# A fused two-block kernel: weight slots of 2,096 words in place of 2,080, so that the second slot begins 64 bytes off its former place modulo 128

## The chip, the cores and the metric

One core of a Trainium2 chip runs one program. The metric is device time in microseconds (us) of one execution; lower is better.

## The reference, cut to what matters

Two transformer blocks run one after the other on 256 tokens of width 1024, all in float32. Nearly all the arithmetic is in products with weight matrices:

```python
proj = rms_norm(x, g) @ w_in                                  # first block: 3 mixers' inputs, gates
mixed = g_a*(o_a @ w_up_a) + g_b*(o_b @ w_up_b) + g_c*(o_c @ w_up_c)
x = x + mixed @ w_out
x = x + (silu(h @ w_gate) * (h @ w_up)) @ w_down              # 1024 -> 2816 -> 1024
...
x = x + 0.5 * swiglu(rms_norm(x), w_gate, w_up, w_down)       # second block: twice, round a mixer
```

The mixers between them (top-k attention, a gated recurrence, latent attention, forgetting attention, stick-breaking attention) are small beside the weights, of which some 185 MB are read.

## The kernel before

The activations stand transposed, 128 features on the partitions and the 256 tokens along the row. The weights come as 189 tiles (`TILES`), most of them 1 MB: 128 partitions by 2,048 words, which is two blocks of 128 output columns by 8 slices of the contraction. The tiles of the down projections (`w_dn`) have 1,408 words, and two of them make one output block. Tile g uses slot g % 2 of three buffers that stand one behind the other in a partition:

```python
SLOT = 4 * FVL                              # L43; FVL = 520, so 2,080 words or 8,320 bytes
raw = fixed("raw", (2, SLOT))               # L352: as loaded
whi = fixed("whi", (2, SLOT), F32R)         # L353: rounded to fp32r
wlo = fixed("wlo", (2, SLOT), F32R)         # L354: raw - whi, what the rounding left
...
mm(bank[:, 0:T], hi, h[:, 0:T], first, False)        # L685: whi x high half of activations
mm(bank[:, 0:T], hi, h[:, T:2 * T], False, False)    # L686: whi x low half
return mm(bank[:, 0:T], lo, h[:, 0:T], False, last)  # L687: wlo x high half
```

SyncE (SP) loads a tile into `raw` (L631) once VectorE has split the tile that had the slot. ScalarE copies `raw` to `whi` (`split_high`, recorded at L1179), in halves, VectorE subtracts into `wlo` (`split_low` L1575, and L1663 in the loops over the gate and up weights), and TensorE then runs three matmuls for each slice of the contraction (`one_region`, all recorded at L681). In nearly all of them the weights are the stationary operand, of 128 columns, and 256 columns of the activations are the moving one (`hs`, `hid`, `ms`, `osplit_a` to `osplit_c`, `osplit_fox`, `osplit_sb`, `cqs`, `ckvs`, `ps`). In five kinds of tiles the roles are exchanged (`block_n`): the weights are streamed, 136 columns at a time (`w_avw`) or 512 (`w_bi`, `w_kvb`, `w_fvl`, `w_sv`), against stationary activations. In `w_avw` and `w_fvl` the rows of a slice have 136 and 520 words, so that four slices running begin 0, 32, 64 and 96 bytes off modulo 128. The last 8 columns of a `w_fvl` slice are stationary in matmuls of their own, 128x8 against 256 moving columns of `hs`.

The order of the work on each engine is written out by hand (`order_of_work`, L194 on), with loops for the gate and up weights (`w_gu`) and the down weights; no place in it depends on `SLOT`.

`fixed` lays tensors out from the lowest free address, each rounded up to 64 bytes. In the built program `x` begins at byte 16,512 of a partition, 129 times 128, and `raw`, `whi` and `wlo` follow at multiples of 128 too. 8,320 is 65 times 128, so slot 1 of each also begins at a multiple of 128. Behind them come `tmp`, `con` and others. The large area of the activations (`arena`) and `hs` begin 64 bytes off modulo 128: all moving operands named above do.

Of the kernel before, what the change touches and what calls it, by code (L numbers as in the profile page):

```python
# [39 lines left out]
LB_FLOOR = 1e-30  # L40
AVW = P + IDX_H
FVL = FOX_H * HD + FOX_H
SLOT = 4 * FVL  # L43
ARENA = 29024


# [283 lines left out]
def build(nc, a, out_t):  # L330

    with ExitStack() as ctx:
# [13 lines left out]
        def fixed(name, shape, dt=F32):  # L346
            off = top[0]
            top[0] += (4 * int(np.prod(shape)) + 63) // 64 * 64
            return at(name, shape, off, dt)

        x = fixed("x", (KD, T))
        raw = fixed("raw", (2, SLOT))  # L352
        whi = fixed("whi", (2, SLOT), F32R)  # L353
        wlo = fixed("wlo", (2, SLOT), F32R)  # L354
        tmp = fixed("tmp", (4, T))
# [1992 lines left out]
```

How the kernel before makes its waits and increments, by code:

```python
        @block.sync  # L613
        def _(sp):
            f, e = FIRST_CONST, EARLY_CONST
            xT = a["xT"].rearrange("k p t -> p k t")
            for piece in range(KD // 2):
                c = slice(2 * piece, 2 * piece + 2)
                sp.dma_start(x[:, c, :], xT[:, c, :]).then_inc(S(f"x_loaded{piece}"), 16)
            sp.dma_start(vec[:], a["vecs"]).then_inc(S("vec_loaded"), 16)
            sp.dma_start(raw[:, 0, 0:TILES[0][2]], a["w_projT_a"][0]).then_inc(S("w_loaded0"), 16)
            half = TILES[1][3]
            sp.dma_start(raw[:, 1, 0:half], a["w_projT_a"][1][:, 0:half]).then_inc(S("w_loaded1a"), 16)
            sp.wait_ge(S(f"x_loaded{KD // 2 - 1}"), 16)
            sp.dma_start(raw[:, 1, half:TILES[1][2]], a["w_projT_a"][1][:, half:]).then_inc(S("w_loaded1"), 16)
            sp.dma_start(con[:, f:e], a["consts"][:, f:e]).then_inc(S("con_loaded"), 16)
            sp.dma_start(con[:, e:], a["consts"][:, e:]).then_inc(S("masks_loaded"), 16)
# [1 line left out]
            def load(src, slot, n, lo_needed):  # L629
                sp.wait_ge(S("w_lo"), lo_needed)
                sp.dma_start(raw[:, slot, 0:n], src).then_inc(S(f"w_loaded{slot}"), 16)
# [8 lines left out]
            def place_bias(tt):  # L640
                sp.wait_ge(S("bias_staged"), tt + 1)
                ks, c0 = P * (tt + 1), P * tt
                for m in range(4):
                    sp.dma_start(bias[m::4, :, c0:c0 + ks], stage[tt][:, ks * m:ks * m + ks])\
                        .then_inc(S("bias_placed"), 16)
```

## Time and profile before

| | us |
|---|---|
| median of three runs | 1059.9 |
| lowest, highest | 1058.3, 1060.31 |
| span of the profiled execution, first to last instruction | 1057.7 |
| median run less that span | 2.2 |
| TensorE busy, of the span | 1047.9 (99%) |
| VectorE busy | 741.0 (70%) |
| ScalarE busy | 579.6 (55%) |
| HBM read | 184.98 MB |

No time of the profiled execution other than its span is among the figures; the 2.2 us stand for what lies around a span. In the profile, "PE" is a matmul and "PEld" the load of a stationary operand, which runs beside the matmul before it. Matmuls are pipelined: each is recorded as some 276 ns long, but the next begins long before that. What counts is the distance from start to start, called spacing here.

### The profile page before, as it was taken

What the parts mean: (1) busy time and instruction counts of PE and PEld (TensorE: products, weight loads), DVE (VectorE), ACT (ScalarE), POOL (GpSimd) and SP (SyncE); (2) the same over time, 40 slices, a digit from 0 to 9 for tenths busy, and PEclk for the clock granted to TensorE, in tenths of its full rate; (3) what the DMA queues carried; (4) which work ended last, traced back from release to release, by engine and by line L of the source; (5) the groups of instructions that cost most, each with busy time, mean ns of one, the idle gap of its engine ahead of it and who ended that gap; (6) DMA issues with size and microseconds to landing.
All of it is one profiled execution on the core that took longest, in us unless ns stands there. A gap on an engine that the chain in (4) does not pass through costs nothing.

```text
span 1057.7 us, 22212 instructions
## 1 busy us (share of the span) xinstructions
PE 1047.9 (99%) x8760; PEld 1020.3 (96%) x8760; DVE 741.0 (70%) x1098; ACT 579.6 (55%) x880; POOL 77.0 (7%) x92
## 2 busy tenths in 40 slices
PE   9999999999999999999999999999999999999998
PEld 8899999999999999999999999898889999999998
DVE  6799988747876666657666677667986876665666
ACT  5456655576565544556544445455666664554553
POOL 0000000001310000111000001041001300000110
PEclk9999999999999999999999999999999999999999
DMA  6356433344556554555555456464335455554563
GB/s 235 129 173 217 162 123 120 120 160 170 190 181 217 190 186 146 198 204 190 205 196 194 148 193 217 173 207 162 137 120 199 171 191 196 198 203 146 195 222 120
DMA packets 32444, 187.81 MB, mean 178 GB/s; under 512 B 3832, under 2 KB 7552, under 8 KB 14720
## 3 DMA queue, kind: packets, MB, share of 16 engines
q1 hardware_dynamic: 31472, 185.58, 50.3%
q0 software_dynamic: 416, 1.06, 0.4%
q8 instruction: 43, 0.70, 0.3%
q10 hardware_dynamic: 496, 0.33, 0.2%
q14 instruction: 17, 0.14, 0.0%
HBM read 184.98 MB, written 1.06 MB: 176 GB/s over the span
## 4 chain that ended last, share of the span: by engine, by line
PE 87%; DVE 6%; ACT 1%; issue 1%; DVEq 0%; ACTq 0%
PE acc L681 83%; PE area_a L681 2%; PE area_t L681 2%; DVE wlo L1575 2%; DVE s_sum L2133 0%; ACT he L1179 0%; ACT whi L1179 0%; PE area_t L947 0%; ACT s_a L1179 0%; DVE mask L1780 0%; DVE st L1765 0%; DVE score L1805 0%; DVE s_z L2135 0%; DVE s_a L2131 0%; DVE s_z L2037 0%
## 5 line engine op out<-in xcount | busy, mean ns | idle before, releaser
L681 PE MATMUL acc<-hs,whi 128*128 128x256 f32 x3584 | 624.6, 279 | 2.9 <-DVE wlo L1575 2.7
L681 PEld LDWEIGHTS acc<-hs,whi 128*128 128x128 f32 x3584 | 541.9, 187 | 10.1 <-issue 7.1
L681 PE MATMUL acc<-hs,wlo 128*128 128x256 f32 x1792 | 496.8, 277 | 0.0
L1179 ACT ACTIVATE whi<-raw 128x1024 fp32r<-128x1024 f32 (+3 forms) x379 | 357.2, 978 | 162.8 <-PE acc L681 136.6
L1575 DVE TENSOR_TENSOR wlo<-raw,whi 128x1024 fp32r<-128x1024 f32 (+4 forms) x259 | 272.1, 1092 | 98.5 <-ACT whi L1179 97.4
L681 PEld LDWEIGHTS acc<-hs,wlo 128*128 128x128 f32 x1792 | 336.1, 188 | 0.2
L681 PE MATMUL acc<-hid,whi 128*128 128x256 f32 x1056 | 180.9, 277 | 0.2 <-DVE wlo L1575 0.2
L681 PEld LDWEIGHTS acc<-hid,whi 128*128 128x128 f32 x1056 | 159.2, 188 | 0.4 <-DVE wlo L1575 0.4
L681 PE MATMUL acc<-hid,wlo 128*128 128x256 f32 x528 | 146.0, 277 | 0.0
L1663 DVE TENSOR_TENSOR wlo<-raw,whi 128x1024 fp32r<-128x1024 f32 x120 | 141.2, 1219 | 4.3 <-ACT whi L1179 4.2
L1676 DVE TENSOR_TENSOR hbuf<-acc,sbuf 128x256 f32<-128x256 f32 x66 | 28.0, 425 | 115.4 <-PE acc L681 112.0
L681 PEld LDWEIGHTS acc<-hid,wlo 128*128 128x128 f32 x528 | 99.1, 188 | 0.0
L1179 ACT ACTIVATE sbuf<-gbuf 128x256 f32<-128x256 f32 x66 | 27.6, 417 | 126.8 <-DVE gbuf L1669 126.8
L681 PE MATMUL acc<-ms,whi 128*128 128x256 f32 x256 | 44.9, 279 | 0.0
L681 PEld LDWEIGHTS acc<-ms,whi 128*128 128x128 f32 x256 | 38.8, 188 | 0.3
L681 PE MATMUL acc<-whi,hs 128*128 128x512 f32 (+1 forms) x128 | 37.4, 370 | 0.0
L2181 POOL TENSOR_TENSOR sq_sum<-sq_sum,sq_ring 128x256 f32<-128x256 f32 x30 | 28.5, 950 | 116.6 <-ACT sq_ring L1179 116.6
L2181 POOL TENSOR_TENSOR sq_sum<-sq_ring 128x256 f32<-128x256 f32 x5 | 5.0, 1000 | 435.2 <-ACT sq_ring L1179 435.2
L2169 POOL TENSOR_TENSOR mixed<-mixed,up 128x256 f32<-128x256 f32 x24 | 17.7, 771 | 250.0 <-DVE up L1605 250.0
L681 PE MATMUL acc<-ms,wlo 128*128 128x256 f32 x128 | 35.5, 278 | 0.0
L1179 ACT ACTIVATE hid<-hbuf 128x256 f32 (+1 forms) x66 | 26.5, 402 | 10.5 <-DVE hbuf L1676 10.5
L1693 DVE TENSOR_TENSOR hid<-hbuf,hid 128x256 f32 (+1 forms) x66 | 27.6, 419 | 2.9 <-ACT hid L1179 2.9
(316 smaller groups left out, 1029.2 us busy)
## 6 DMA issues: line engine op xcount, KB each, us to landing
raw<-in_w_gu SPq DMA_DIRECT2D x66, 1024.0 KB, 4.8
raw<-in_w_dn SPq DMA_DIRECT2D x48, 704.0 KB, 4.0
raw<-in_w_up SPq DMA_DIRECT2D x10, 1024.0 KB, 4.8
raw<-in_w_gates1b SPq DMA_DIRECT2D x8, 1024.0 KB, 4.7
raw<-in_w_out SPq DMA_DIRECT2D x8, 1024.0 KB, 4.8
raw<-in_w_qk SPq DMA_DIRECT2D x8, 1024.0 KB, 4.8
raw<-in_w_gates SPq DMA_DIRECT2D x8, 1024.0 KB, 4.8
raw<-in_w_projT_b SPq DMA_DIRECT2D x7, 1024.0 KB, 4.8
```

The costliest lines, as they stand in the source:

```text
L681: return nc.tensor.matmul(out, w, m, start=start, stop=stop, skip_group_check=True)
L1179: return nc.scalar.activation(out, in_, f, **kw)
L1575: m = v.tensor_tensor(to, src, hi.bitcast(F32), ALU.subtract)
L1663: v.tensor_tensor(wlo[:, 1 - j, c], raw[:, 1 - j, c], whi[:, 1 - j, c].bitcast(F32), ALU.subtract).then_inc(S("w_lo"), 1)
L1676: v.tensor_tensor(hbuf[:, j, :], acc[(n0 + 2 * j + 1) % 4][:, 0:T], sbuf[:, j, :], ALU.mult)\
L1693: v.tensor_tensor(hid[:, t - 1, T:2 * T], hbuf[:, 1 - j, :], hid[:, t - 1, 0:T].bitcast(F32), ALU.subtract).then_inc(S("hid_lo"), 1)
L2169: nc.gpsimd.tensor_tensor(mixed[:, k, :], mixed[:, k, :], up[:, u % 4, :], ALU.add)\
L2181: nc.gpsimd.tensor_tensor(sq_sum[:], before, sq_ring[:, k % 2, :], ALU.add)\
```

## The change

It makes a slot of the three buffers 16 words (64 bytes) longer. Nothing reads or writes the new words.

```diff
@@ -40,7 +40,7 @@
 LB_FLOOR = 1e-30
 AVW = P + IDX_H
 FVL = FOX_H * HD + FOX_H
-SLOT = 4 * FVL
+SLOT = 4 * FVL + 16
 ARENA = 29024
```

A slot is then 8,384 bytes, 65.5 times 128. Slot 0 of `raw` stays; slot 0 of `whi` moves up by 128 bytes and that of `wlo` by 256; all that is behind them moves by 384. Those keep their places modulo 128. Slot 1 of each of the three alone is now 64 bytes off modulo 128, which is the place of `hs` and of the activations in the arena. The instructions of every engine, their number and their order are the same in both programs.

## Rows read from the trace of the kernel before

**Rows 1.** The page: busy time, share of the span, instructions; granted TensorE clock.
```profile
PE 1047.9 (99%) x8760; PEld 1020.3 (96%) x8760; DVE 741.0 (70%) x1098; ACT 579.6 (55%) x880; POOL 77.0 (7%) x92
PEclk9999999999999999999999999999999999999999
```

**Rows 2.** The chain of waits in order of time: start us, us, what, matmuls.
```profile
118.70 5.89 PE acc L681 x48
126.38 5.66 PE acc L681 x48
133.82 5.66 PE acc L681 x48
...
303.48 174.80 PE acc L681 x1536
...
851.47 180.61 PE acc L681 x1584
```

**Rows 3.** Windows: us, each engine's busy time (x instructions), granted clock, DMA share, GB/s.
```profile
304.00:314.00 10.00, 10.00 (x87) 10.00 (x86) 8.29 (x10) 6.64 (x9) 0.00 (x0) 1.00 0.50 193
...
326.00:416.00 90.00, 90.00 (x797) 90.00 (x796) 56.77 (x85) 44.86 (x66) 0.00 (x0) 1.00 0.53 188
```

**Rows 4.** Timeline of TensorE matmuls, 313.9 to 315.2 us: start us, us, what.
```profile
313.92 0.40 PE L681 MATMUL acc<-hs,whi 128*128 128x256 f32 x2
...
314.27 0.40 PE L681 MATMUL acc<-hs,whi 128*128 128x256 f32 x2
...
314.62 0.39 PE L681 MATMUL acc<-hs,whi 128*128 128x256 f32 x2
...
314.96 0.39 PE L681 MATMUL acc<-hs,whi 128*128 128x256 f32 x2
```

**Rows 5.** Groups of instructions by line and form: count, busy us, mean ns.
```profile
L681 PE MATMUL acc<-hs,whi 128*128 128x256 f32 x3568 | 621.7, 279 | 2.9 <-DVE wlo L1575 2.7
L681 PE MATMUL acc<-hs,wlo 128*128 128x256 f32 x1784 | 494.6, 277 | 0.0
L681 PE MATMUL acc<-hid,whi 128*128 128x256 f32 x1056 | 180.9, 277 | 0.2 <-DVE wlo L1575 0.2
L681 PE MATMUL acc<-hid,wlo 128*128 128x256 f32 x528 | 146.0, 277 | 0.0
```

**Rows 6.** Timeline of TensorE matmuls: the 8-column weights of w_fvl, two places.
```profile
667.56 0.39 PE L681 MATMUL acc<-hs,whi 128*8 128x256 f32 x2
...
667.91 0.39 PE L681 MATMUL acc<-hs,whi 128*8 128x256 f32 x2
...
671.05 0.39 PE L681 MATMUL acc<-hs,whi 128*8 128x256 f32 x2
...
671.39 0.39 PE L681 MATMUL acc<-hs,whi 128*8 128x256 f32 x2
```

**Rows 7.** Groups by line and form: loads of stationary weights, 128 and 8 columns.
```profile
L681 PEld LDWEIGHTS acc<-hs,whi 128*128 128x128 f32 x3568 | 540.5, 188 | 9.1 <-issue 7.1 <-DVE wlo L1575 1.0 <-DVE qk L1607 0.2
...
L681 PEld LDWEIGHTS acc<-hs,whi 128*8 128x8 f32 x16 | 1.4, 88 | 1.0
```

**Rows 8.** Timeline of TensorE matmuls with weights moving, 512 columns, w_bi: aligned slices.
```profile
102.36 0.62 PE L681 MATMUL acc<-whi,hs 128*128 128x512 f32 x2
...
103.05 0.62 PE L681 MATMUL acc<-whi,hs 128*128 128x512 f32 x2
...
107.17 0.63 PE L681 MATMUL acc<-whi,hs 128*128 128x512 f32 x2
...
107.87 0.63 PE L681 MATMUL acc<-whi,hs 128*128 128x512 f32 x2
```

**Rows 9.** The same view in w_fvl, where slices begin 0, 32, 64, 96 bytes off.
```profile
665.23 0.63 PE L681 MATMUL acc<-whi,hs 128*128 128x512 f32 x2
...
665.93 0.63 PE L681 MATMUL acc<-whi,hs 128*128 128x512 f32 x2
...
666.63 0.62 PE L681 MATMUL acc<-whi,hs 128*128 128x512 f32 x2
```

**Rows 10.** One line's instructions: duration ns min/median/max; first and last start.
```profile
L1663 DVE TENSOR_TENSOR wlo<-raw,whi x120: 1216/1218/1227, 311.8 to 962.3; 128x1024 fp32r<-128x1024 f32 x120
```

**Rows 11.** DMA issues by tensor: count, KB each, median us from issue to landing.
```profile
raw<-in_w_gu SPq DMA_DIRECT2D x66, 1024.0 KB, 4.8
raw<-in_w_dn SPq DMA_DIRECT2D x48, 704.0 KB, 4.0
...
raw<-in_w_kvb SPq DMA_DIRECT2D x1, 1024.0 KB, 4.7
...
raw<-in_w_pp SPq DMA_DIRECT2D x1, 1024.0 KB, 4.7
```

**Rows 12.** Timeline of TensorE: transposes in plain fp32, 128 columns.
```profile
751.75 0.49 PE L947 MATMUL area_t<-con,f_p 128*128 128x128 f32 x3
```

## The prediction

> **What bounds the kernel now.** The page first: TensorE is busy for 1047.9 us of a span of 1057.7, at the full granted clock, the higher of its two levels (2.4 GHz), in every slice [rows 1]. A busy TensorE is not yet a bound, so the chain of waits comes next. It is made of runs of matmuls at line L681 that nothing interrupts: 1,536 of them in 174.80 us, 1,584 in 180.61 [rows 2]. VectorE and ScalarE are busy 70% and 55% and stand on the chain only between those runs. So the time is the number of matmuls times their spacing, plus the gaps of the mixers. The change touches no instruction; what it can alter is how fast an instruction reads or writes at its new address, and TensorE's spacing above all.
>
> The third view is that spacing. It has two values. From 326 to 416 us TensorE issues 797 matmuls in 90 us, 113 ns each; from 304 to 314 us it issues 87 in 10 us, 115 ns by count, and a few records can be missing, so the timeline is surer [rows 3]. There three matmuls (one slice) start 0.35 us after the last three up to 314.62, and 0.34 from then on [rows 4]. Over longer stretches of the same form: 48 matmuls in 5.66 us at 126.38 and 133.82, 118 ns each [rows 2]. I call them slow and fast: 118 and 113.3 ns. The reader is to see three things. The spacing changes inside an unbroken stream, at the border of a tile. It then stays: within the 90 us of fast spacing both slots were used in turn, and VectorE and ScalarE came and went (85 and 66 instructions) without moving it. And slot 1 (at 126.38, tile 17) and slot 0 (at 133.82, tile 18) both show the slow one. So what picks the spacing is neither the slot nor the neighbours; it is some phase that is set when TensorE has waited or turned to another tile.
>
> How much runs at each: of the two long runs of the chain, 1,536 in 174.80 us is 113.8 ns each and 1,584 in 180.61 is 114.0 [rows 2], so a tenth to a sixth of them is slow. In the short runs between the mixers most is, like the two of 48. I take a quarter of all as slow. The number of matmuls that matter is 3,568 + 1,784 + 1,056 + 528 = 6,936 [rows 5], and some 900 with `ms`, `osplit` and the small ones; 7,800 in all, 3,900 of them in slot 1.
>
> **The change part by part.** *Instructions:* none added, removed or moved, 0.
>
> *VectorE and ScalarE on slot 1.* They read `raw` and `whi` and write `wlo`, all three shifted by the same 64 bytes. The subtraction takes 1,216 to 1,227 ns over 120 instances, half of them in each slot [rows 10], while TensorE reads the other slot at whatever address. With the operands' places relative to each other unchanged I take 0. If each of the 188 halves that pass through slot 1 grew by 1%, 12 ns, it would be 2 us of VectorE's time, and its 30% of idle time [rows 1] covers them; without that cover they would be TensorE's.
>
> *The loads.* A tile lands 4.8 us after its issue, one of `w_dn` after 4.0 [rows 11]. Tile 23 (`w_kvb`) goes to slot 1 and tile 188 (`w_pp`) to slot 0; today these begin 128 bytes apart modulo 256, and both took 4.7 us [rows 11]. I take 0, and 5% of 4.0 us as the dearest case for the 24 tiles of `w_dn` in slot 1, 33 matmuls or 3.7 us apart, where the load has the least cover: 0.2 × 24 = 4.8 us. The page "DMA: Bandwidth & Descriptors" of the Trainium skill, section "How a descriptor splits into AXI transactions", has a read that does not start at a multiple of 256 bytes begin at the boundary below it. It speaks against the change, since slot 1 of `raw` leaves such a boundary; but slot 0 lies off one already, and the two rows above agree to 0.1 us, so the sum by the page would be the same here.
>
> *TensorE, weights moving* (`w_avw`, `w_bi`, `w_kvb`, `w_fvl`, `w_sv`). Here the trace shows other addresses. With aligned slices, three matmuls of 512 columns take 0.69 us at 102.36 and 0.70 at 107.17 [rows 8], again two values. In `w_fvl`, where the slices begin at 0, 32, 64 and 96 bytes, three take 0.70 and 0.70 [rows 9]. So all four places lie at the upper of the two values that one place alone has, and the 64 bytes make at most 0.01 us per three. There are some 130 such matmuls in slot 1: 0 taken, 0.4 us either way as the bound.
>
> *TensorE, weights stationary.* This is the term that decides, 3,900 matmuls in slot 1. The trace has no 128-column weights at 64 bytes off, so it is bounded. The nearest rows are the 8-column weights of `w_fvl`: their load takes 88 ns in place of 188 [rows 7], it reads a sixteenth of the words, and still the spacing of their matmuls is 0.35 us per three at one place and 0.34 at the next [rows 6], the same two values as with full weights. If the 6 to 11 ns above the 107 ns of the transposes [rows 12] came from the weights' reads meeting the activations' reads, they ought to have shrunk there. They did not; so I take it that they belong to the moving operand, whose address modulo 128 the change leaves alone. I take 0 because these rows are nearest. Above, the bound is that all of slot 1 goes slow: three quarters of 3,900 by (118 - 113.3) = 4.7 ns, +13.7 us. Below, that all of it goes fast: a quarter of 3,900 by 4.7, -4.6 us. Farther below, that the excess vanishes in slot 1: three fp32 transposes take 0.49 us in all, of which the last one's own 0.28 is to be taken off, so that they start some 107 ns apart [rows 12]; 3,900 × 6.3 ns and the slow ones' 4.6 make -29 us.
>
> The page "TensorE: Matmul & The Clock Gate" of the Trainium skill, section "Back-to-back issue gap", gives 256/2.4 + 2.5 = 109.2 ns for a warm matmul. The trace has 113.3 at best, so there is an excess of 4 ns that the page does not explain; if the change removed it in slot 1 the page's figure would make the sum 3,900 × 4.1 = 16 us shorter.
>
> *Sum:* 1057.7 + 0 = 1057.7 us of span, and with the 2.2 around it 1059.9, the median of the runs shown.
>
> **The rivals.** A measurement of this kernel tells 0.2%, 2.1 us, from no change: that is the width of its three runs.
>
> *Slower: slot 1 favours the slow phase.* Every weight load of an odd tile would read in the same place modulo 128 in which its matmul streams `hs` or `hid`. For it: in the fast stretch all operands keep 64 bytes between them, and the spacing is so even that reads do seem to lie in a pattern. Against it: the 8-column rows. Complete, it gives +13.7, 1073.6 us; as tiles alternate, a phase found anew at each of 188 borders costs some 13 ns each as a minimum, 2.5 us, 1062.4. It decides once over 450 of the 2,900 fast matmuls in slot 1 turn slow (450 × 4.7 ns = 2.1 us). Chance 0.19.
>
> *Faster: slot 1 favours the fast phase, or drops part of the excess.* For it: phases exist and are set at tile borders, so another address may set them otherwise. Against it: a quarter is all there is to win. -4.6, 1055.3 us; chance 0.18, of which 0.03 for the excess itself going, down to 1031.
>
> *Slower by the loads:* up to +4.8, 1064.7 us, if a write at 64 bytes off takes 5% longer and `w_dn` has no cover. Chance 0.03.
>
> *The change does nothing it says:* 8,384 bytes are 65.5 × 128, so it does; the others' places modulo 256 move as well (`whi` by 128), and slots 0 and 1 differ by that today without a difference in spacing. This gives the forecast's time too, and has no chance of its own.
>
> **How the numbers follow.** No effect has 0.60, at 1059.9 us. Faster 0.18, within 0.2% 0.60, slower 0.22. The range runs from 1054, below the faster case, to 1068, over the load case and half of the way of the slower one; what it leaves out is the upper half of that one and the excess going, some 0.12, and a part of the spread of each. Both signs are not most of the chance, so no second range stands here.
>
> **What would show it.** Right: the long stretches of `w_gu` again 113.3 ns apart in tiles of both slots, a chain of 174.8 and 180.6 us for the same counts, L1663 again at 1,218 ns, loads at 4.8 us. Wrong: a spacing that alternates with the tile, 24 or 48 matmuls of one kind and as many of the other; that would mean that the stationary weights' address modulo 128 against the activations' does count, and that the excess over 107 ns is shared between the two reads. A slower load would show in ScalarE's waits for `raw`.

## The result, and the profile after

The changed kernel takes 1074.67 us (median of 4 runs, 1073.2 to 1076.59), the kernel before 1059.5 beside it: a ratio of 1.0143, 95% interval 1.0128 to 1.0159. The change makes the kernel slower by 1.4%. The forecast said 1059.9, no change, and its range ended at 1068; what came is the rival "slot 1 favours the slow phase", for which the text had 1073.6 us and a chance of 0.19.

The page of the profiled execution after (span 1074.0 us; busy us, share, instructions; granted clock), against [rows 1]:

```profile
PE 1064.0 (99%) x8760; PEld 1037.1 (97%) x8760; DVE 742.5 (69%) x1098; ACT 579.8 (54%) x880; POOL 75.9 (7%) x92
PEclk9999999999999999999999999999999999999999
```

TensorE is busy for 16.1 us more, with as many matmuls, at the same granted clock (full speed, the 2.4 GHz level). The span grew by 16.3. VectorE is busy for 1.5 us more and ScalarE for 0.2. The subtraction on the shifted tiles, against [rows 10], and the loads, against [rows 11]:

```profile
L1663 DVE TENSOR_TENSOR wlo<-raw,whi x120: 1215/1218/1227, 312.6 to 976.7; 128x1024 fp32r<-128x1024 f32 x120
```
```profile
raw<-in_w_gu SPq DMA_DIRECT2D x66, 1024.0 KB, 4.8
raw<-in_w_dn SPq DMA_DIRECT2D x48, 704.0 KB, 4.1
```

The median is 1,218 ns as before and a load lands after 4.8 and 4.1 us (4.8 and 4.0 before). So it is TensorE's spacing that has to be looked at. By groups of line and form, against [rows 5]:

```profile
L681 PE MATMUL acc<-hs,whi 128*128 128x256 f32 x3568 | 633.7, 281 | 2.9 <-DVE wlo L1575 2.4 <-DVE hs L1718 0.4
L681 PE MATMUL acc<-hs,wlo 128*128 128x256 f32 x1784 | 498.4, 279 | 0.0
L681 PE MATMUL acc<-hid,whi 128*128 128x256 f32 x1056 | 184.8, 279 | 0.3 <-DVE wlo L1575 0.3
L681 PE MATMUL acc<-hid,wlo 128*128 128x256 f32 x528 | 147.4, 279 | 0.0
```

Each group is 2 ns a matmul longer, 281 for 279 and 279 for 277, and the idle time before the first is 2.9 us in both. Nothing waits that did not wait before. What a group's mean cannot show is which matmuls are the longer ones. The chain of waits shows it (start us, us, what, matmuls), against [rows 2]:

```profile
118.70 5.94 PE acc L681 x48
126.43 5.68 PE acc L681 x48
133.90 5.46 PE acc L681 x48
...
304.30 184.07 PE acc L681 x1584
489.23 119.78 PE acc L681 x1008
...
863.92 184.07 PE acc L681 x1584
```

In the kernel before, the tile at 126 us (slot 1) and the one at 134 us (slot 0) took 5.66 us each. Now slot 1 takes 5.68 and slot 0 takes 5.46: the faster of the two is the one that the change left at its distance. The long run from 863.92 has 1,584 matmuls in 184.07 us, 116.2 ns each, where [rows 2] had the same 1,584 in 180.61, 114.0. The timeline near the start of the first `w_gu` stream gives the pattern. These rows are the first matmuls of four tiles in turn (the third to the sixth of the stream), 48 matmuls apart (start us, us, what):

```profile
309.82 0.28 PE L681 MATMUL acc<-hs,whi 128*128 128x256 f32 x1
...
315.26 0.40 PE L681 MATMUL acc<-hs,whi 128*128 128x256 f32 x2
...
320.94 0.28 PE L681 MATMUL acc<-hs,whi 128*128 128x256 f32 x1
...
326.38 0.40 PE L681 MATMUL acc<-hs,whi 128*128 128x256 f32 x2
```

5.44, 5.68 and 5.44 us: 113.3 ns a matmul in slot 0, 118.3 in slot 1, 113.3 in slot 0, and it goes on so through the stretch that was evenly fast before [rows 3]. That is the sign that the prediction named for being wrong, a spacing that alternates with the tile. The starts in the two timelines, taken tile by tile, give the mean spacing of each stream (ns a matmul, from the first matmul of a tile to its last; `w_gu` without its first two tiles, in which TensorE waits) and how much later each stage begins than before:

```
                slot 0   slot 1    before 0 / 1      later at the stage's start
w_gu0            113.3    118.3    113.8 / 113.3     +0.8 us (297 us)
w_dn0            113.8    119.1    113.9 / 113.9     +3.0    (418 us)
w_gu1            119.1    118.3    114.0 / 113.3     +4.2    (478 us)
w_dn1            113.9    119.5    113.9 / 115.2     +9.0    (600 us)
mixers behind                                        +10.3   (661 us)
w_gu2            113.3    118.3    113.8 / 113.3     +12.4   (845 us)
w_dn2            113.8    119.1    113.9 / 113.9     +14.7   (966 us)
end of the span                                      +16.3
```

The three `w_gu` streams lose 2.3, 4.8 and 2.3 us and the three `w_dn` streams 1.2 to 1.3 each, 13.1 in all; the mixers and the rest lose 3.2. One line stands out: in `w_gu1` slot 0 is slow too, over its whole length, though the change did not touch slot 0's distance to `hs` modulo 128. That comes back below.

### The profile page after: what moved, and what is told of

It reads as the page before. It is cut to its first block, busy times and chain, and to the rows that moved or that the text cites. A ratio compares the mean times of both kernels' runs of the same rounds, so it can differ in the third digit from the quotient of the medians.

```text
span 1074.0 us, 22212 instructions
## 1 busy us (share of the span) xinstructions
PE 1064.0 (99%) x8760; PEld 1037.1 (97%) x8760; DVE 742.5 (69%) x1098; ACT 579.8 (54%) x880; POOL 75.9 (7%) x92
## 4 chain that ended last, share of the span: by engine, by line
PE 87%; DVE 7%; ACT 2%; issue 1%; DVEq 0%; ACTq 0%
PE acc L681 82%; PE area_a L681 2%; PE area_t L681 2%; DVE wlo L1575 2%; ACT whi L1179 0%; DVE s_sum L2133 0%; ACT he L1179 0%; PE area_t L947 0%; ACT s_a L1179 0%; DVE mask L1780 0%; DVE st L1765 0%; DVE score L1805 0%; DVE s_z L2135 0%; DVE s_a L2131 0%; DVE s_z L2037 0%
## 5 line engine op out<-in xcount | busy, mean ns | idle before, releaser
L681 PE MATMUL acc<-hs,whi 128*128 128x256 f32 x3584 | 636.7, 281 | 2.9 <-DVE wlo L1575 2.4
L681 PE MATMUL acc<-hid,whi 128*128 128x256 f32 x1056 | 184.8, 279 | 0.3 <-DVE wlo L1575 0.3
L1663 DVE TENSOR_TENSOR wlo<-raw,whi 128x1024 fp32r<-128x1024 f32 x120 | 141.1, 1218 | 3.7 <-ACT whi L1179 3.7
```

What stands on the lines that cost most here:

```text
L681: return nc.tensor.matmul(out, w, m, start=start, stop=stop, skip_group_check=True)
L1663: v.tensor_tensor(wlo[:, 1 - j, c], raw[:, 1 - j, c], whi[:, 1 - j, c].bitcast(F32), ALU.subtract).then_inc(S("w_lo"), 1)
```

## The experiments

The question is what about an address costs 5 ns. For each slot the text gives the **distance**, the address of the activations less that of the weights. In the kernel before, `whi` and `wlo` begin at 0 modulo 128 in both slots and `hs` and `hid` at 64, so the distance is 64 modulo 128 in both slots. The change makes it 0 in slot 1. Modulo 256 the distance of `hs` was 64 in slot 0 and 192 in slot 1 before, and that of `hid` 192 in slot 0 and 64 in slot 1. "Before" in each comparison is the kernel before on the same chip. Spacings are from the timelines' starts, tile by tile, unless a row is shown.

### A shift by 128 bytes: modulo 128 as before

```diff
-SLOT = 4 * FVL
+SLOT = 4 * FVL + 32
```

> A slot is 32 words longer than before (128 bytes, twice the change), so slot 1 is back at a multiple of 128. Theory A (the weights' place modulo 128 against the activations' place is what counts; the same place is slow): no change, 1059.5 us within 2, both slots 113.3 ns apart in the fast stretches. Rival B (a longer slot, or the shift of what lies behind it, costs by itself): about 1075 us or more.

1073.02 us (1072.64 to 1074.19), ratio 1.0126 [1.0110, 1.0143]. The distance modulo 128 alone, which is as before here, would give no change, so it is not the whole account. Its chain of waits:

```profile
304.54 184.37 PE acc L681 x1584
489.78 118.98 PE acc L681 x1008
```

The timeline's starts give 117.8 ns in both slots over all of `w_gu0`, `w_gu1` and `w_gu2`, and 113.3 in `w_dn0` and `w_dn2`. These are exactly the two values of the kernel before, but a stream that began slow stayed slow. So the slow phase of [rows 4] has a price of its own when nothing ends it. (`w_dn1` is mixed: its first tile slow, the next eight at 113.3, the last seven 117.8. It turned both times right behind a wait of TensorE.)

### Activations moved instead of weights

```diff
-        base = top[0]
+        base = top[0] + 64
```

`base` is where the arena with `hid` and `hs` begins, so this leaves every weight where it was and makes the distance 0 modulo 128 in both slots.

> Slots as before (both at multiples of 128), but the arena and hs, with all activations that stream through TensorE, moved up by 64 bytes, so that they too begin at multiples of 128. Theory A (equal places modulo 128 are slow): now both slots are slow, 118.4 to 119 ns everywhere; 7,800 matmuls by some 4 ns over the mean of before, about 1090 us. Rival C (weights that begin at 64 modulo 128 are slow by themselves, wherever the activations are): no change, 1059.5 us. Rival D (a difference between the two slots costs, since TensorE has to find a new phase at every border): no change, 1059.5 us.

1093.37 us (1093.14 to 1093.61), ratio 1.0321 [1.0303, 1.0338]. The chain:

```profile
308.45 188.91 PE acc L681 x1584
498.23 120.37 PE acc L681 x1008
```

118.5 to 119.9 ns in nearly every tile of both slots. The weights lie where they lay, and it costs more than twice what the change costs: it is not the weights' own place that counts. It could be the activations' own place, or the distance; the next kernel tells these two apart.

### Both together

```diff
-SLOT = 4 * FVL
+SLOT = 4 * FVL + 16
...
-        base = top[0]
+        base = top[0] + 64
```

> The change (slots 16 words longer) and the arena and hs moved up by 64 bytes too: slot 0 and the activations at multiples of 128, slot 1 64 bytes off. Theory A: as slow as the change, about 1075 us, but the slots have changed roles: slot 0 118.4 to 119 ns, slot 1 113.3. Rival C: slot 1 stays the slow one. Rival D: about 1075 us with either slot slow.

1077.2 us (1076.95 to 1077.46), ratio 1.0166 [1.0149, 1.0183]. In the `w_gu` streams the slots change roles, 118.3 ns in slot 0 and 113.7 in slot 1, as the distance says: activations at a multiple of 128 bytes run fast there once the weights stand 64 off. In the `w_dn` streams they do not: 119.1 and 118.8, though slot 1 has the distance 64 there as well. This half was not explained.

### The raw weights alone

```diff
-        raw = fixed("raw", (2, SLOT))
+        raw = fixed("raw", (2, SLOT + 16))
```

> Only raw has the longer slots; whi and wlo keep theirs. Theory A: TensorE never reads raw, so no change, 1059.5 us within 2. Rival E (the loads into raw at 64 bytes off, or ScalarE and VectorE reading it, slow the kernel): slower by part or all of 15 us.

1059.31 us (10 runs), ratio 0.9999 [0.9989, 1.0008]. The loads into `raw` at 64 bytes off, and ScalarE's and VectorE's reads of it there, cost nothing, as the prediction had it.

### Which of the other two: the high or the low weights alone

```diff
-        whi = fixed("whi", (2, SLOT), F32R)
+        whi = fixed("whi", (2, SLOT + 16), F32R)
```

> Only whi has the longer slots: in slot 1 the high weights (two of three loads of a slice) stand in the activations' place modulo 128, the low weights do not. If each load that coincides costs by itself: two thirds of the change's 15 us, about 1069.5 us. If one bad load of three is enough to lose the fast phase: 1075 us. Cost by slot 1 alone.

1075.28 us (1075.18 to 1075.85), ratio 1.0152 [1.0135, 1.0169]: all of the change's cost with two of the three weight loads of a slice at the bad distance.

```diff
-        wlo = fixed("wlo", (2, SLOT), F32R)
+        wlo = fixed("wlo", (2, SLOT + 16), F32R)
```

> Only wlo has the longer slots: in slot 1 one of three loads of a slice stands in the activations' place modulo 128. whi alone cost all of the change's 15 us. If one bad load of three is enough: 1073 to 1076 us again. If the cost goes by the number of bad loads: 5 to 8 us, 1065 to 1068.

1080.2 us (1080.02 to 1080.91), ratio 1.0202 [1.0185, 1.0219]. One bad load of three costs more than the change does. Their chains from the start of `w_gu0` on, first the high weights', then the low weights':

```profile
304.58 184.94 PE acc L681 x1584
```
```profile
304.94 186.34 PE acc L681 x1584
```

116.8 and 117.6 ns a matmul. With the low weights alone slot 0 is slow as well, 117.8 in all three `w_gu` streams, where all its distances are 64. With the high weights alone it is so in `w_dn` only (118.8, and 114.0 in `w_gu`). So the cost is not a sum over loads: a stretch of matmuls at a bad distance also decides how the good ones behind it run.

### Other distances

```diff
-        base = top[0]
+        base = top[0] + 32
```

> Slots as before, activations moved up by 32 bytes: activations less weights is 96 modulo 128 in both slots, a place between the good one (64) and the bad one (0). Theory A/F: between, or like 64 if the bad places are those within 64 bytes of each other: 1060 to 1091 us; I take 1075. A rival by which only an exact coincidence is bad: 1051 to 1060.

1092.49 us (1092.39 to 1092.58), ratio 1.0313 [1.0295, 1.0330]: distance 96, 118.1 to 120.1 ns.

```diff
-        base = top[0]
+        base = top[0] + 96
```

> Slots as before, activations moved up by 96 bytes: activations less weights is 32 modulo 128 in both slots, the last of the four places (0 and 96 gave 118.2 to 120 ns, 1092 to 1093 us; 64 the fast one). If only 64 has a fast phase: no 113.3 anywhere, 1088 to 1094 us. If 32 is on the good side: 1059 or below.

1079.39 us (1079.27 to 1079.55), ratio 1.0192 [1.0175, 1.0209]: distance 32, 116.6 to 118.8 ns.

```diff
-        base = top[0]
+        base = top[0] + 128
```

> Slots as before, activations moved up by 128 bytes: the differences modulo 256 (64 in slot 0 and 192 in slot 1 for hs, the other way for hid) change places, those modulo 128 stay 64. Theory F: the long streams fast again, the switch to fast in the gate/up tiles one tile earlier or later; 1059.5 within 4. Rival G: the same, or some streams slow.

1060.14 us (1058.9 to 1060.54), ratio 1.0004 [0.9995, 1.0014]: distance 64 again, 113.3 ns from the second to the fifth tile of a stream on. Of the four distances modulo 128 that were tried only 64 has 113.3 ns. At 32 and 96 only the activations were moved, so that there the distance and the activations' own place are not told apart.

### Does one value modulo 256 choose the fast phase?

With 128 bytes between the slots the distance of `hs` is 64 modulo 256 in both, that of `hid` 192; the first experiment had `w_gu` slow and `w_dn` fast, which looks like a rule. Here every distance is 192:

```diff
-SLOT = 4 * FVL
-ARENA = 29024
+SLOT = 4 * FVL + 32
+ARENA = 29024 + 32
```

> Slots 32 words longer (as e1) and the arena 32 words longer, so that weights of both slots stand at 128 modulo 256 and every streamed activation (hs too) at 64 modulo 256: activations less weights is 192 modulo 256 everywhere. In before, every switch inside a stream from 118 to 113 ns came on entering a tile with that difference, and in e1, whose gate/up tiles have 64 in both slots, all of them ran at 117.8, the down tiles (192) at 113.3. Theory F (the difference modulo 256 picks the phase: 192 the fast one, 64 the slow one or the one that was there, 0 and 128 always slow): nearly all at 113.3, 1051 us, 8 below before. Rival G (the phase is picked by chance at each start, modulo 128 alone counts): anywhere between 1059 and 1075, with some streams at 117.8.

1063.84 us, ratio 1.0030 [1.0004, 1.0055], and ten runs between 1057.1 and 1070.03, where the kernel before stays within 1.6 us beside it. The chain:

```profile
304.50 179.79 PE acc L681 x1584
485.15 114.74 PE acc L681 x1008
...
850.88 186.56 PE acc L681 x1584
```

113.5 and 113.8 ns a matmul in the first two, 117.8 in the third, in one execution of one program: `w_gu2` has the distances of `w_gu0` to the byte, and is slow throughout. So the distance modulo 256 does not choose the phase. The six streams show both phases, each nearly from end to end (`w_gu0` and `w_gu1` turned within their first three tiles, right behind waits of TensorE), and the spread of the runs fits a phase that is set by chance.

### Is it a jump that ends the slow phase?

In the kernel before, `whi` and `wlo` move by 128 modulo 256 at each change of slot, and its slow streams turned fast at a tile's border [rows 4]. In the two kernels above with long slow streams they don't move, and of their twelve streams only three turned at all (`w_dn1` of the first, `w_gu0` and `w_gu1` of the second), each time right behind a wait. If a jump does it, more jumps might be better. This puts one at each slice, on the activations' side:

```diff
-        hs = at("hs", (KD, 2 * T), hs_off, F32R)
+        hs = at("hs", (KD, 2 * T + 32), hs_off, F32R)
...
-        hid = arena("hid", 4096, (KF, 2 * T), F32R)
+        hid = arena("hid", 4096, (KF, 2 * T + 32), F32R)
```

> Slots as before; the rows of hs and hid get 32 words between one slice of the contraction and the next, so the activations' place alternates by 128 bytes modulo 256 with every slice, while the difference modulo 128 stays 64. Where the difference never alternates (e1, x1) a stream kept the spacing it began with, 117.8 or 113.3, over hundreds of matmuls; where it alternates from tile to tile (before, s_act_128) every slow stream turned fast within three tiles. Theory H (a jump of 128 bytes knocks a stream out of the slow phase and leaves the fast one alone): with a jump at each slice hs and hid streams are at 113.3 after a slice or two, about 1054 us. Rival I (frequent jumps cost themselves, or hold a stream in a mixture): spacing over 114 in the long streams, 1060 to 1090 us.

1074.71 us (1074.44 to 1076.0), ratio 1.0152 [1.0135, 1.0169], and 116.8 to 117.0 ns in nearly every tile. Its chain:

```profile
303.86 185.22 PE acc L681 x1584
```

A jump at each slice keeps the stream from ever running at 113.3. By the starts, three matmuls of a slice take some 354 ns where the distance modulo 256 is 64 and 346 where it is 192, in turn; the steady phases have 353 and 340. What is left is a jump that comes seldom. The next kernels move the weights by 128 bytes in the middle of each tile (`HALF`); the splits of ScalarE and VectorE are shifted with them:

```diff
+HALF = 32
+SLOT = 4 * FVL + HALF
...
-                            block_t((g0 + j) % 2, b * KD * P, KD, n0 + 2 * j + b, hs)
+                            block_t((g0 + j) % 2, b * (KD * P + HALF), KD, n0 + 2 * j + b, hs)
```

> The second half of each weight tile in whi and wlo stands 128 bytes further, and slots are 8,448 bytes apart, so that the place of the weights jumps by 128 modulo 256 at each half of a tile (24 matmuls) and not only at each tile; modulo 128 everything stays 64 from the activations. Theory H' (a jump of the weights by 128 modulo 256 at a border lets a slow stream turn fast, and costs a fast one nothing, as before and s_act_128 show at the borders of tiles): slow streams last half as long, 1055 us, 4 below before. Rival K (what turned them was the border of a tile itself, with any jump absent as in e1 and x1 made up for by chance): as x1, 1057 to 1070 and spread wide. Rival I' (each jump costs, as in x2): 1062 to 1075 us with small spread.

1057.22 us (1056.87 to 1057.84), ratio 0.9983 [0.9973, 0.9992]. With the activations 128 bytes later as well:

> As h1_halves with the activations 128 bytes further, so that first and second halves of a tile change roles modulo 256. Theory H': 1055 us within 3, the turn to fast half a tile earlier or later. Rival K and I' as for h1_halves.

1055.81 us (1055.56 to 1056.6), ratio 0.9970 [0.9959, 0.9981]. With the jump in the middle of a tile and none between tiles (`SLOT = 4 * FVL + 2 * HALF`):

> As h1_halves with slots 8,576 bytes apart, so that the weights jump by 128 modulo 256 in the middle of each tile and not at its border. Theory H': one jump per tile as in before, only elsewhere: 1059 us, long streams at 113.3. Rival K (the border of a tile is what counts): like x1 and e1, whole streams at 117.8 in some runs.

1058.16 us (1057.62 to 1059.36), ratio 0.9990 [0.9980, 0.9999]. All three leave out part of the computation: the first tile of each `w_dn` is split in the `w_gu` loop, which cuts at the eighth slice and not at the sixth, so two slices of it were read where nothing fresh had been written. The first two are therefore repeated with the cut of `w_dn` at the eighth slice, which computes all:

```diff
-    add("w_dn0", 16, KF * P // 2, 6 * P)
+    add("w_dn0", 16, KF * P // 2, 8 * P)
...
-                            block_t((g + part) % 2, 0, 6, n, hid, half * part, part == 0, False)
+                            block_t((g + part) % 2, 0, 8, n, hid, half * part, part == 0, False)
...
-                            m = block_t((g + part) % 2, 6 * P, 5, n, hid, half * part + 6, False, part == 1)
+                            m = block_t((g + part) % 2, 8 * P + HALF, 3, n, hid, half * part + 8, False, part == 1)
```

> h2_halves_128 again (low and high weights 32 words further in the second half of every slice tile, activations 128 bytes later), with the down tiles cut at their eighth slice instead of at the sixth, because the first down tile is split in the gate/up loop, which cuts at the eighth, so that there h2 left two slices of three tiles unshifted where TensorE reads them shifted: part of the sum was computed from stale weights, and h5 computes all of it. Theory H' (a jump of the weights by 128 modulo 256 lets a slow stream turn fast, whatever the numbers are): 113.3 ns from the second or third tile of each stream, 1054.5 to 1057.5 us, ratio 0.996 to 0.998. Rival L (h1 to h3 were quicker because of the stale weights, or the later cut costs what the jump gives): 1059 to 1061 us.

1056.99 us (1056.15 to 1057.96), ratio 0.9979 [0.9970, 0.9988].

> The same without the 128 bytes on the activations (h1_halves with the down tiles cut at the eighth slice). Theory H': one to three tiles per stream slower than in h5_halves_8_128, as h1 against h2, 1056 to 1058.5 us, ratio 0.997 to 0.999. Rival L: 1059 to 1061 us.

1058.3 us (1058.0 to 1058.68), ratio 0.9988 [0.9979, 0.9997].

> The kernel before with the down tiles cut at the eighth slice and nothing else changed: what that cut alone is worth. Theory H': nothing, 1058.5 to 1060.5 us, ratio 0.999 to 1.001, since both halves of a tile are split long before TensorE wants them. Rival L: either a loss of some 1 us that would hide part of the jump's gain, or a gain that would be the cut's own and not the jump's (under 0.998).

1059.77 us (1059.55 to 1060.69), ratio 1.0004 [0.9995, 1.0013]: the cut alone is worth nothing. The chains of the two kernels, first with the jump in the middle of a tile and the 128 bytes, then with the cut alone:

```profile
302.48 174.35 PE acc L684 x1536
```
```profile
303.51 174.80 PE acc L681 x1536
```

113.5 against 113.8 ns. With the jumps `w_gu0`, `w_gu1` and `w_gu2` are in the fast phase from their first tile on, and run at 113.3 wherever nothing waits; without them the first three tiles of each are in the slow one. This is the version of the study that beats both kernels, by 0.2%, near the edge of what can be told. What the jump does is also bounded: `w_dn` still begins with one to three tiles that are slow in whole or in part, and in the kernel without the 128 bytes `w_dn2` went back from 113.3 to 117.8 behind a wait in its fourth tile, until its sixth began.

Where exactly do the streams turn? Here are the starts of five slices in turn in the fifth tile of `w_gu1`, in the kernel with the jump in the middle of a tile only. The middle of the tile, its 25th matmul, is at 504.37:

```profile
503.31 0.40 PE L684 MATMUL acc<-hs,whi 128*128 128x256 f32 x2
...
503.66 0.40 PE L684 MATMUL acc<-hs,whi 128*128 128x256 f32 x2
...
504.01 0.40 PE L684 MATMUL acc<-hs,whi 128*128 128x256 f32 x2
...
504.37 0.39 PE L684 MATMUL acc<-hs,whi 128*128 128x256 f32 x2
...
504.71 0.39 PE L684 MATMUL acc<-hs,whi 128*128 128x256 f32 x2
```

The slices are 0.35 or 0.36 us apart up to there and 0.34 from there on; in the kernel before the turn stands at the border of a tile [rows 4]. The traces of the nine kernels with such jumps (before, the raw weights alone, the activations 128 bytes later, the five with `HALF`, the cut alone) have 46 turns from slow to fast that no wait stands before, the first two tiles of `w_gu` left out. All 46 are where the weights' jump takes the distance modulo 256 from 64 to 192, or one slice behind it: at the border of a tile, at its 25th or, where `w_dn` is cut at the sixth slice, its 19th matmul, whichever the kernel has. None is at a jump from 192 to 64. Not every jump to 192 turns the stream. The turns back from fast to slow, with the same tiles left out, are four, three in these nine kernels and one in the first with 128 bytes more a slot; each stands at a slice that a wait had made at least 60 ns longer. So the rule tried above was half right: a distance of 192 does not choose the fast phase, but a slow stream that nothing interrupts turned fast only at a jump to it.

### Does a narrower weight load show the cost?

The prediction leaned on the 8-column weights of [rows 6]. This is the changed kernel with 8-column weights in the `w_gu` and `w_dn` loops, the first two tiles of each `w_gu` excepted (it leaves out 120 of 128 outputs of each block there):

```diff
+            def block_s(slot, c0, n_k, n, h, k0=0, first=True, last=True):
...
+                    m = one_region(acc[n % 4][0:8, :], whi[:, slot, c:c + 8], wlo[:, slot, c:c + 8], h[:, k0 + k, :],
```

> The changed kernel with stationary weights of 8 columns in place of 128 in the loops over the gate/up and down tiles; it leaves out 120 of 128 output columns there, and serves for the spacing alone. The prediction's reason (the excess over 107 ns belongs to the moving operand, since it stands with 8-column weights too): both slots alike, 113 to 118 ns. Theory J (the excess of slot 1 is where the weights' reads meet the activations'): with a sixteenth of the reads slot 1 loses its extra, both slots at 113.3 or less, toward 107 to 109.

1071.45 us (one run). The groups of weight loads (busy us, mean ns) and the chain:

```profile
L681 PEld LDWEIGHTS acc<-hs,whi 128*128 128x128 f32 x1648 | 252.0, 188 | 8.6 <-issue 6.2 <-DVE wlo L1583 1.7
L681 PEld LDWEIGHTS acc<-hs,whi 128*8 128x8 f32 x1936 | 170.1, 88 | 53.0
```
```profile
304.50 183.39 PE acc L681 x1584
```

The load falls from 188 to 88 ns, and the spacing hardly: in `w_gu` 113.4 in slot 0 and 116.5 in slot 1, still 3.1 above it, where the full loads had 5.0. In `w_dn` it is 116.7 and 117.7, where the full loads had 113.8 and 119.1; why slot 0, at the good distance, is slower there with narrow loads was not explained. In `w_gu` a load that reads a sixteenth of the words keeps most of the dependence on where it reads. So "it did not shrink with the number of words" does not mean "it does not come from the load's place".

## Why the prediction was wrong

**What bounds the kernel** was right: TensorE is busy for 99% of the span in both kernels, the span grew by 16.3 us and its busy time by 16.1.

**The phases** were right in their sizes (113.3 and 117.8 ns return in nearly every experiment) and in that they persist. The text was wrong to conclude from the evenly fast 90 us of [rows 3] that "what picks the spacing is neither the slot nor the neighbours". Those rows show only that it made no difference while both slots had the same distance modulo 128. In all of them the distance was 64 modulo 128. And the turns that the text put down to the border of a tile stand at one kind of border, that at which the distance modulo 256 goes to 192.

**VectorE, ScalarE, the loads**: taken at 0, and 0 they are (ratio 0.9999 with the raw weights alone).

**Weights moving** was taken at 0 and bounded at 0.4 us, and the two traces bear it out: the starts of the matmuls with 512 moving columns are 234.7 ns apart on average before and 234.0 after (gaps over 0.4 us left out), those with 136 columns 112.9 in both. So the mixers' 3.2 us are not theirs; the short streams of stationary weights are what is left.

**Weights stationary** is the step that failed. It said that the excess over 107 ns ought to have shrunk for 8-column weights if it came from the weights' reads meeting the activations' reads, that it had not, and that therefore the change would cost 0. The narrow experiment shows the inference false: in `w_gu`, with 8-column loads, the bad distance still costs 3.1 ns over the good one. Narrow loads need not lose the dependence on their address, so that a spacing which stands with them too says nothing about that dependence. The change at the full width then cost 5.0 ns a matmul in `w_gu` and 5.3 in `w_dn` against slot 0, where the step had 0.

Worse, [rows 6] had the answer in them. By the layout of a `w_fvl` slice the 8-column weights of the slice at 667.56 begin 64 bytes off, at distance 0 from `hs`, and those at 671.05 at a multiple of 128, at distance 64. The first takes 0.35 us (349 ns by the starts) and the second 0.34 (341). The text read them as the two phases; read by the distance they are the bad and the good one. In the kernel with the activations moved by 64 bytes the first slice of the same second tile, now at distance 0, takes 348 ns and the one whose weights begin 64 bytes off takes 342. These are single slices, and another at distance 64, at 663.41 in slot 0, takes 354, as the slow phase would have it: the rows could have raised the chance of the other case, not shown it. The 107 ns, too, are a little low: the starts of the transposes of [rows 12] are 109 ns apart.

The upper bound of the same step, +13.7 us, was the right size by a partly wrong count. It had three quarters of 3,900 matmuls in slot 1 at 4.7 ns. Measured in the feed-forward streams: 2,376 in slot 1 at 4.6 ns on average, 10.8 us; 0.2 us given back in slot 0, where early tiles are now fast; and 2.4 us for the 528 of `w_gu1` in slot 0 (4.6 ns each), which no case had. The mixers' 3.2 us make the rest of 16.3. That the sum came so near the bound is in part luck. The price of the other unknown, the excess vanishing (1031 us), never came near: no kernel of the 18 ran a long stream under 113.3 ns.

**The chances.** The text gave the forecast 0.60 though its rows had one distance modulo 128 only for weights of full width, and those of [rows 6] were read as phases. With the deciding operand so little varied, the two bounds of the sum (-4.6 and +13.7) deserved more of the chance and the range should have reached the upper one, which the same paragraph had worked out.

**Against the Trainium skill.** The page "TensorE: Matmul & The Clock Gate", section "Step-by-step: what each phase is for", says that TensorE has two independent read ports and that loading the next weights takes no read bandwidth from the running matmul. The runs here speak against independence as a rule for timing: moving the activations alone by 64 bytes, with no instruction changed, costs 3.2%. The 109.2 ns that the prediction worked out for 256 columns, from the same page's section "Back-to-back issue gap", was not reached by any stream; the best was 113.3.

**What is shown, and what stays open.** Shown: the cost is TensorE's, and neither the loads nor the raw weights have a part in it; it depends on where weights and activations stand relative to each other modulo 128 (in the `w_gu` streams, where either side was moved and both together); 64 is the only one of 0, 32, 64 and 96 that has 113.3 ns; at 64 there are two phases that can last for a whole stream. Shown by where the turns stand, in nine kernels: a slow stream turns fast where the weights' jump takes the distance from 64 to 192 modulo 256, or behind a wait. Not shown: what the two reads meet in (that it is a conflict of reads at all is a guess that fits), why only some of these jumps turn a stream, why a shifted slot can hold its neighbour in the slow phase in one stream (`w_gu1`) and not in the others, and why `w_dn` did not follow the distance when both sides were moved. Distances of 16 and 48 were not tried.

## What to carry to other kernels

When one kernel streams matmuls whose two operands both come from SBUF, the pair of addresses is a parameter: try the moving operand at 0, 32, 64 and 96 bytes from the stationary one modulo 128 before tuning anything finer, since in this kernel it was worth 3.2%. Padding that keeps the distance modulo 128 is not enough: 128 bytes more a slot cost 1.3%, and went with a distance modulo 256 that no longer changed from slot to slot. Even rows from a stretch in which an operand's place never varies say nothing about that place: give such an unknown the whole width of its bounds. And before reading two values as noise or phases, work out the address behind each row. Compare spacing tile by tile, because a group's mean hid 5 ns in every second tile behind 2 ns.

## What the runs showed of the hardware that was not expected

- The spacing of 256-column matmuls with 128x128 weights depends on the distance of their operands modulo 128: 113.3 or 117.8 ns where every load stands at 64, 118.3 to 119.9 at 0, 118.1 to 120.1 at 96, 116.6 to 118.8 at 32.
- Two phases, 113.3 and 117.8 ns, can each last over a thousand matmuls at the same distances: 1,584 in 179.79 us and 1,584 in 186.56 us in one execution.
- A jump of 128 bytes in the activations at every slice gives 116.9 ns throughout, while a jump in the weights in the middle of each tile gives 113.3.
- All 46 turns from 117.8 to 113.3 ns that no wait stands before are where the distance goes from 64 to 192 modulo 256; the four turns back inside a stream each stand at a wait.
- With `wlo` alone shifted, one load of three at the bad distance costs 2.0%, more than all three together (1.4%).
- Weight loads of 8 columns take 88 ns for 188, but bring the spacing at the bad distance only from 118.3 to 116.5 in `w_gu`, and at the good one not below 113.3.
